# The last layer norm of a two-block transformer kernel: an extra bank, the root on other engines, smaller stores

## The chip, the core and the metric

One NeuronCore of a Trainium2 chip runs the whole program. The metric is the time of one execution on the device in microseconds (us). The engines are TensorE (PE, its weight loads PEld), VectorE (DVE), ScalarE (ACT), GpSimd (POOL) and SyncE (SP), which here only issues DMAs.

## The reference

A first transformer block and then two layers of a second one, on 256 tokens of width 1024, in float32. The second block's layers end with a gated feed-forward part and a layer norm; the change concerns only the last of these norms, the one whose result is the output.

```python
def layer_norm(x, g, b):
    mu = jnp.mean(x, axis=-1, keepdims=True)
    var = jnp.mean(jnp.square(x - mu), axis=-1, keepdims=True)
    return (x - mu) * lax.rsqrt(var + LN_EPS) * g + b

for l in range(2):
    ...
    x = layer_norm(ALPHA * x + 0.5 * swiglu(x, ffn2_w_in[l], ffn2_w_out[l]), ln_g[l, 2], ln_b[l, 2])
return x
```

## The kernel before

The 256 tokens are two tiles t=0 and t=1 of 128, tokens on the partitions. `xres` holds the residual, 128 x 2 x 1024. Every product of float32 matrices is made of three matmuls, high part by high part, high by low and low by high (`tile_mm`, L1555 to L1563), so `whi`/`wlo` are the parts of a weight block and `ht_hi`/`ht_lo` those of the hidden values. PSUM is one tensor `ps` of eight banks of 128 x 512; banks 4 to 7 gather the feed-forward output: bank 4+2t+h is tile t, columns half h. Banks 2, 3, 0 and 1 take the up projections (`up_unit`).

The program is written engine by engine, each with its own instruction stream; the order is by hand and semaphores join them. At the end of a feed-forward part `ffn_pe` finishes tile 0, then tile 1; of each it first adds the last but one unit of weights to both halves, then the last unit to half 0 and half 1. After each finished bank it raises `y_done`, after the very last one `used`. Where another norm follows, a function `late` puts transposes in front of the last product; for the last norm it is None.

`norm_dve` (L1291) is VectorE's part. For a tile, `add` (L1302) adds a bank of PSUM onto `xres` and writes the row sums to `sums`; an instruction with such a sum shows as two, the second being DVE_READ_ACCUMULATOR. `mean` (L1307) makes the negative mean `nmean` and raises `mean_ready`; `centre` (L1312) makes `cent` = (x - mean) g; `scale` (L1319) waits for `lrs`, multiplies and adds `ln_b`, in halves of 512 columns, and raises `xt_src` after each. The order is add, add, mean, centre, scale for tile 0 and then the same for tile 1. ScalarE (`norm_act`, L856) squares x - mean with a row sum into `mv`. GpSimd (`norm_pool`, `rsqrt`, L551 and L553) makes `lrs` from it: multiply and add, drain, power -0.5. ScalarE's last work before the norm are the two activations L900 of `ffn_act`. SP waits for `xt_src` and stores each half of a tile (L485, 256 KB), then waits for all four.

Of the kernel before, what the change touches and what calls it, by code (L numbers as in the profile page):

```python
# [8 lines left out]
P = 128  # L9
TOK = 256  # L10
TT = TOK // P
DM = 1024
KD = DM // P
# [9 lines left out]
LAYERS = 2  # L23
# [17 lines left out]
BW = 512  # L41
# [53 lines left out]
AHEAD = 6  # L95
ATT_ROPES = {0: (P_DQ, 0), 2: (P_DQ, 1), 4: (P_DK, 0), 6: (P_DK, 1)}
# [61 lines left out]
def build(nc, x, positions, ln1_g, w_in, q_norm_a, k_norm_a, q_norm_b, k_norm_b, sinks, w_branch_a,  # L158
# [19 lines left out]
    with ctx:  # L178
# [88 lines left out]
        nmean = little("nmean", [P, TT])  # L267
        mv = little("mv", [P, TT, 2])
# [91 lines left out]
        stored = sem("stored")  # L360
        up_tile = sem("up_tile")
# [78 lines left out]
        def _(sp):  # L440
# [40 lines left out]
            for t in range(TT):  # L481
                for h in range(2):
                    cols = slice(h * BW, (h + 1) * BW)
                    sp.wait_ge(xt_src, 4 * (XT1 + 4 * LAYERS) + 2 * t + h + 1)
                    sp.dma_start(out_r[:, t, cols], xres[:, t, cols]).then_inc(stored, 16)  # L485
            sp.wait_ge(stored, 32 * TT)
# [79 lines left out]
        def _(pool):  # L566
# [4 lines left out]
            pool.memset(half[:, :], -0.5)  # L571
            pool.memset(one_lam[:, :, :], 1.0)
# [35 lines left out]
            for l in range(LAYERS):  # L608
# [7 lines left out]
                norm_pool(pool, q + 2)  # L616
# [241 lines left out]

        def hidden_act(act, g, u, ffn):
# [43 lines left out]
        def _(act):  # L903
# [83 lines left out]
            for l in range(LAYERS):  # L987
# [49 lines left out]
                ffn_act(act, u + L_FFN2, g + FFN_S, 2 * l + 1, () if last else (u + L_UNITS, u + L_UNITS + 1))  # L1037
                for t in range(TT):
                    norm_act(act, 3 * l + 2, t)
                    if not last:  # L1040
                        xt_act(act, n + 4, toks=(t,))
# [249 lines left out]
        def norm_dve(dve, q, n, y, u, ffn, last=False):  # L1291
# [39 lines left out]
            if not last:  # L1331
                xt_dve(dve, n, toks=(0,), banks=banks, halves=(0,))
            centre(1)
            if not last:
                xt_dve(dve, n, toks=(0,), banks=banks, halves=(1,))
            scale(1)
            if not last:
                xt_dve(dve, n, toks=(1,), banks=banks)
# [48 lines left out]
        def _(dve):  # L1387
# [118 lines left out]
            for l in range(LAYERS):  # L1506
# [46 lines left out]
                norm_dve(dve, q + 2, n + 4, y + 5, u + L_UNITS - 1, True, last)  # L1553
# [407 lines left out]

        def ffn_pe(pe, u, g, f, n, late=None, banks=XT_BANKS):
# [11 lines left out]
            for t in range(TT):  # L1974
# [8 lines left out]
                for h in range(2):  # L1983
                    for k in range(2):
                        if t == h == k == 1 and late is not None:
                            late()
                        m = down_tile(pe, end, k, h, t, False, k == 1, k, par)
# [173 lines left out]
```

## Time and profile before

| | |
|---|---|
| median of 3 runs | 1321.42 us (1321.1 to 1323.9) |
| span of the profiled execution | 1321.2 us |
| PE busy | 99% of the span |
| DVE, ACT, POOL busy | 70%, 49%, 5% |
| DMA | 238.11 MB, mean 180 GB/s |
| granted clock of PE | 0.997 of full speed |

The span runs from the first to the last instruction of the profiled execution, so it is compared with the runs directly. Matmuls are pipelined: the difference of two starts is what one costs, and its own time is longer. The rows on which the prediction rests stand in a section further down.

### The profile page before, as it was taken

The numbers are of one execution on the slowest core, as the hardware profiler recorded it, in microseconds if no ns is written. First come the engines' busy times: TensorE is split into PE (matmuls) and PEld (weight loads), VectorE is DVE, ScalarE is ACT, GpSimd is POOL, SyncE is SP. The second block draws the span as 40 slices with busy tenths as digits, with TensorE's granted clock in tenths as the row PEclk, the third lists the DMA queues.
The fourth block names the chain that finished last, engine by engine and source line by source line (L and its number), as shares of the span: only waits on it lengthen the run. The fifth ranks groups of instructions, "written<-read, shape, count | busy, mean of one in ns | idle before, by whom it ended". The sixth has DMA issues, their size and how long they took to land.

```text
span 1321.2 us, 17217 instructions
## 1 busy us (share of the span) xinstructions
PE 1306.3 (99%) x6973; PEld 1102.8 (83%) x6973; DVE 925.2 (70%) x1188; ACT 640.9 (49%) x839; POOL 70.0 (5%) x145
## 2 busy tenths in 40 slices
PE   8999999999999999999999999999999999999997
PEld 7887788888888888887888888888888877888886
DVE  6698777766656666788876666776666888676665
ACT  6777635443335444457554444444443566544441
POOL 4121000000000000000300000000000003000000
PEclk9999999999999999999999999999999999999999
DMA  8543565555555555653565555465555444655550
GB/s 303 192 159 87 138 238 166 190 193 190 194 208 199 191 191 191 191 145 100 171 223 191 192 191 190 154 236 193 187 193 186 160 128 127 231 190 192 188 188 33
DMA packets 155167, 238.11 MB, mean 180 GB/s; under 512 B 4248, under 2 KB 110768, under 8 KB 155088
## 3 DMA queue, kind: packets, MB, share of 16 engines
q1 hardware_dynamic: 154704, 236.47, 54.7%
q8 instruction: 55, 0.90, 0.3%
q0 software_dynamic: 384, 0.54, 0.2%
q14 instruction: 24, 0.20, 0.0%
HBM read 235.95 MB, written 1.05 MB: 179 GB/s over the span
## 4 chain that ended last, share of the span: by engine, by line
issue 86%; PE 10%; POOL 2%; POOLq 1%; ACT 1%; DMA 0%; DVE 0%; SPq 0%; DVEq 0%; ACTq 0%
PE ps L1561 2%; PE ps L1563 2%; PE ps L1562 2%; POOLq L552 1%; POOL drs L553 1%; PE ps L1705 1%; PE ps L1628 1%; POOL lrs L553 1%; PE ps L1714 0%; DMA raw<-in_w_in_dram 0%; PE ps L1729 0%; ACT ebuf L734 0%; PE ps L1683 0%; PE ps L1603 0%; PE ps L1604 0%
## 5 line engine op out<-in xcount | busy, mean ns | idle before, releaser
L527 DVE TENSOR_TENSOR wlo<-raw,whi 128x2048 fp32r<-128x2048 f32 x172 | 391.8, 2287 | 129.2 <-ACT whi L519 129.2
L519 ACT ACTIVATE whi<-raw 128x2048 fp32r<-128x2048 f32 x197 | 369.8, 1905 | 22.3 <-DMA raw<-in_w_up_dram 11.1
L1924 PE MATMUL ps<-xt_both,whi 128*128 128x512 f32 x1504 | 358.7, 390 | 0.0
L1924 PEld LDWEIGHTS ps<-xt_both,whi 128*128 128x128 f32 x1504 | 279.1, 188 | 55.9
L1929 PEld LDWEIGHTS ps<-xt_both,wlo 128*128 128x128 f32 x1504 | 193.4, 191 | 7.6
L1241 DVE TENSOR_REDUCE hid_a<-ps 128x512 f32<-128x1024 f32 (+1 forms) x98 | 115.3, 1177 | 119.5 <-PE ps L1929 119.3
L1929 PE MATMUL ps<-xt_both,wlo 128*128 128x256 f32 x1504 | 195.7, 283 | 0.0
L1561 PE MATMUL ps<-whi,ht_hi 128*128 128x512 f32 x480 | 187.7, 391 | 0.0
L1562 PE MATMUL ps<-wlo,ht_hi 128*128 128x512 f32 x480 | 187.3, 390 | 0.0
L1563 PE MATMUL ps<-whi,ht_lo 128*128 128x512 f32 x480 | 186.8, 389 | 0.0
L877 ACT ACTIVATE hid_b<-hid_a 128x512 f32<-128x512 f32 x40 | 25.2, 631 | 236.5 <-DVE hid_a L1241 236.5
L1561 PE MATMUL ps<-whi,xt_both 128*128 128x512 f32 (+1 forms) x288 | 112.8, 392 | 0.0
L1562 PE MATMUL ps<-wlo,xt_both 128*128 128x512 f32 (+1 forms) x288 | 109.0, 378 | 0.0
L1563 PE MATMUL ps<-whi,xt_both 128*128 128x512 f32 (+1 forms) x288 | 109.0, 378 | 0.0
L1563 PEld LDWEIGHTS ps<-whi,ht_lo 128*128 128x128 f32 x480 | 90.1, 188 | 19.1
L1561 PEld LDWEIGHTS ps<-whi,ht_hi 128*128 128x128 f32 x480 | 90.3, 188 | 17.4
L1562 PEld LDWEIGHTS ps<-wlo,ht_hi 128*128 128x128 f32 x480 | 90.3, 188 | 16.8
L892 ACT ACTIVATE ht_hi<-hid_b 128x512 fp32r<-128x512 f32 x36 | 22.8, 633 | 94.1 <-DVE hid_b L1264 94.1
L500 DVE SCALAR_TENSOR_TENSOR wlo<-raw,g_cols,whi 128x512 fp32r<-128x512 f32 x80 | 56.1, 767 | 13.9 <-ACT whi L493 13.9
L1561 PEld LDWEIGHTS ps<-whi,xt_both 128*128 128x128 f32 x288 | 54.2, 188 | 12.0 <-issue 2.7
L1563 PEld LDWEIGHTS ps<-whi,xt_both 128*128 128x128 f32 x288 | 54.2, 188 | 10.4
L1562 PEld LDWEIGHTS ps<-wlo,xt_both 128*128 128x128 f32 x288 | 54.3, 189 | 8.6
(233 smaller groups left out, 1340.6 us busy)
## 6 DMA issues: line engine op xcount, KB each, us to landing
raw<-in_ffn_w_in_dram SPq DMA_DIRECT2D x80, 1024.0 KB
raw<-in_ffn_w_out_dram SPq DMA_DIRECT2D x44, 1024.0 KB
raw<-in_w_in_dram SPq DMA_DIRECT2D x36, 1024.0 KB
raw<-in_w_up_dram SPq DMA_DIRECT2D x16, 1024.0 KB
raw<-in_w_down_dram SPq DMA_DIRECT2D x16, 1024.0 KB
raw<-in_w_out_dram SPq DMA_DIRECT2D x8, 1024.0 KB
raw<-in_ffn_w_in_dram SPq DMA_DIRECT2D x16, 512.0 KB
raw<-in_w_out_dram SPq DMA_DIRECT2D x8, 512.0 KB
```

The costliest lines, as they stand in the source:

```text
L500: m = dve.scalar_tensor_tensor(wlo[j][:, cols], raw[j][:, cols], g_cols[:, k:k + 1], whi[j][:, cols].bitcast(F32), ALU.mult, ALU.subtract)
L519: act.activation(whi[j][:, :], raw[j][:, :], ACT.Copy).then_inc(hi_done, 1)
L527: dve.tensor_tensor(wlo[j][:, :], raw[j][:, :], whi[j][:, :].bitcast(F32), ALU.subtract).then_inc(lo_done, 1)
L553: pool.tensor_tensor(dst, dst, half[:, 0:dst.shape[-1]], ALU.pow).then_inc(done, 1)
L877: act.activation(hid_b[:, 0, :], hid_a[:, 0, :], ACT.Silu).then_inc(hid_act, 2)
L892: act.activation(ht_hi[s % 2][:, 0:2, :], hidden2, ACT.Copy).then_inc(ht_hi_done, 2)
L1241: return dve.tensor_reduce(hid_a[:, j, k * TOK:(k + n) * TOK].rearrange("p (k n) -> p k n", k=n), ps[:, b:b + n, :].rearrange("p k (j n) - ...
L1561: pe.matmul(o, hi[:, k, tok], block_of(whi, u, b, width), start=start, stop=False)
L1562: pe.matmul(o, hi[:, k, tok], block_of(wlo, u, b, width), start=False, stop=False)
L1563: return pe.matmul(o, lo[:, k, tok], block_of(whi, u, b, width), start=False, stop=stop)
L1924: pe.matmul(o(k).rearrange("p (j n) -> p j n", j=2), whi[w][:, block(b, k)], xt_both[:, :, b, :], start=b == 0, stop=False)
L1929: m = pe.matmul(o(k)[:, 0:TOK], wlo[w][:, block(b, k)], xt_hi[:, b, :], start=False, stop=b == KD - 1)
```

## The change

Only the last norm (layer 1, second feed-forward part) changes.

- TensorE: the last product (tile 1, half 1, last unit of weights) is done in two quarters of 256 columns. The first goes on in bank 7 and raises `y_done`, the second starts anew in bank 0 and raises `used`; it is the only one for its columns in that bank, so bank 7 holds what came before it.
- VectorE has a function of its own. Of tile 1 it adds 512 columns, 256 and 256 from bank 6 and 7, sums two quarters' totals, and adds the 256 columns from bank 0 last, whose total replaces that of the third add. A mean divided by 32 as well goes to ScalarE; a second instruction makes the mean proper. `factor` waits for `var_ready` and takes a reciprocal in place of the wait for GpSimd.
- ScalarE squares with scale 1/32, so that the sum is the variance, drains, and takes the root with `eps2` as bias. A small Sqrt stands ahead of both tiles.
- GpSimd sets the constant `eps2` and leaves out its last `norm_pool`.
- Stores: five pieces, two of tile 0 (512 columns each), three of tile 1 (512, 256 and 256 columns), each waiting for `rows_out`.

```diff
+LAST_PIECES = ((0, slice(0, BW)), (0, slice(BW, DM)), (1, slice(0, BW)), (1, slice(BW, DM - BW // 2)),
+               (1, slice(DM - BW // 2, DM)))
...
-            for t in range(TT):
-                for h in range(2):
-                    cols = slice(h * BW, (h + 1) * BW)
-                    sp.wait_ge(xt_src, 4 * (XT1 + 4 * LAYERS) + 2 * t + h + 1)
-                    sp.dma_start(out_r[:, t, cols], xres[:, t, cols]).then_inc(stored, 16)
-            sp.wait_ge(stored, 32 * TT)
+            for i, (t, cols) in enumerate(LAST_PIECES):
+                sp.wait_ge(rows_out, i + 1)
+                sp.dma_start(out_r[:, t, cols], xres[:, t, cols]).then_inc(stored, 16)
+            sp.wait_ge(stored, 16 * len(LAST_PIECES))
...
+            pool.memset(eps2[:, :], EPS2 / ALPHA ** 2)
...
-                norm_pool(pool, q + 2)
+                if l < LAYERS - 1:
+                    norm_pool(pool, q + 2)
...
+        def last_norm_act(act, q, t):
+
+            act.wait_ge(mean_ready, 2 * q + t + 1)
+            act.activation(squares[:, t, :], xres[:, t, :], ACT.Square, bias=nmean_root[:, t:t + 1], scale=1.0 / ROOT_DM,
+                           accum_out=mv[:, t, 1:2])
+            act.drain()
+            act.activation(lrs[:, t:t + 1], mv[:, t, 1:2], ACT.Sqrt, bias=eps2[:, 0:1]).then_inc(var_ready, 1)
...
+                if last:
+                    act.activation(scratch[:, :], ident[:, 0:1], ACT.Sqrt)
                 for t in range(TT):
-                    norm_act(act, 3 * l + 2, t)
-                    if not last:
+                    if last:
+                        last_norm_act(act, 3 * l + 2, t)
+                    else:
+                        norm_act(act, 3 * l + 2, t)
                         xt_act(act, n + 4, toks=(t,))
...
+        def last_norm_dve(dve, q, y, u):
+
+
+            def add(t, a, z, src, total, *ready):
+                xs = xres[:, t, a:z]
+                dve.wait_ge(*ready)
+                dve.scalar_tensor_tensor(xs, src, 0.5 / ALPHA, xs, ALU.mult, ALU.add, accum_out=total)
+
+            def mean(t, first, second):
+                dve.drain()
+                dve.tensor_scalar(nmean_root[:, t:t + 1], first, second, -1.0 / (DM * ROOT_DM),
+                                  ALU.add, ALU.mult).then_inc(mean_ready, 1)
+                dve.tensor_scalar(nmean[:, t:t + 1], first, second, -1.0 / DM, ALU.add, ALU.mult)
+                dve.drain()
...
+            def factor(t):
+                dve.wait_ge(var_ready, 2 * q + t + 1)
+                m = dve.reciprocal(lrs[:, t:t + 1], lrs[:, t:t + 1])
+                dve.drain()
+                return m
+
+            def scale(t, cols):
+                dve.scalar_tensor_tensor(xres[:, t, cols], cent[:, t, cols], lrs[:, t:t + 1], ln_b[:, cols],
+                                         ALU.mult, ALU.add).then_inc(rows_out, 1)
...
+            centre(0)
+            factor(0)
+            for t, cols in LAST_PIECES[:2]:
+                scale(t, cols)
+            add(1, 0, BW, ps[:, 6, :], quarter[:, 0:1], y_done, y + 3)
+            add(1, BW, DM - BW // 2, ps[:, 7, 0:BW // 2], quarter[:, 1:2], y_done, y + 4)
+            add(1, DM - BW // 2, DM, ps[:, 7, BW // 2:BW], quarter[:, 3:4], y_done, y + 4)
+            dve.drain()
+            dve.tensor_tensor(quarter[:, 2:3], quarter[:, 0:1], quarter[:, 1:2], ALU.add)
+            add(1, DM - BW // 2, DM, ps[:, 0, 0:BW // 2], quarter[:, 3:4], used, u + 1)
+            mean(1, quarter[:, 2:3], quarter[:, 3:4])
+            centre(1)
+            dve.drain()
+            factor(1)
+            for i, (t, cols) in enumerate(LAST_PIECES[2:]):
+                scale(t, cols)
...
+        def last_columns(pe, u, par):
+
+            tok = slice(P, TOK)
+            for q, o in enumerate((ps[:, 7, 0:BW // 2], ps[:, 0, 0:BW // 2])):
+                for k in range(2):
+                    a = (2 * k + 1) * BW + q * BW // 2
+                    hi, lo = (w[SLOT_OF[u]][:, a:a + BW // 2] for w in (whi, wlo))
+                    pe.matmul(o, ht_hi[par][:, k, tok], hi, start=q == 1 and k == 0, stop=False)
+                    pe.matmul(o, ht_hi[par][:, k, tok], lo, start=False, stop=False)
+                    m = pe.matmul(o, ht_lo[par][:, k, tok], hi, start=False, stop=k == 1)
+                m.then_inc(y_done if q == 0 else used, 1)
...
+                    if t == h == 1 and late is None:
+                        last_columns(pe, end, par)
+                        break
```

## Rows read from the trace of the kernel before

**Rows 1.** The page, part 1: busy time, share and instructions of each engine.

```profile
PE 1306.3 (99%) x6973; PEld 1102.8 (83%) x6973; DVE 925.2 (70%) x1188; ACT 640.9 (49%) x839; POOL 70.0 (5%) x145
```

**Rows 2.** Busy time by stretch, for PE, PEld, DVE, ACT, POOL; then clock, DMA share, GB/s.

```profile
1314.00:1317.30 3.30, 0.00 (x1) 0.00 (x0) 2.31 (x6) 1.24 (x2) 0.69 (x2) 0.87 0.37 138
1317.30:1321.20 3.90, 0.00 (x0) 0.00 (x0) 1.41 (x2) 0.00 (x0) 0.05 (x1) 0.50 0.37 137
```

**Rows 3.** The chain of work that ended last: start, us, what.

```profile
1316.78 0.58 POOLq L178
...
1317.38 0.75 DVE xres L1319
```

**Rows 4.** The timeline of PE: start, us, engine, line, operation; the last six matmuls.

```profile
1312.48 0.39 PE L1561 MATMUL ps<-whi,ht_hi 128*128 128x512 f32 x1
...
1313.61 0.39 PE L1563 MATMUL ps<-whi,ht_lo 128*128 128x512 f32 x1
```

**Rows 5.** The timeline of DVE, with idle time before in brackets.

```profile
1312.17 1.41 DVE L1319 SCALAR_TENSOR_TENSOR xres<-cent,lrs,ln_b 128x512 f32<-128x512 f32 x2 [1.20 <-POOL lrs L553]
1313.51 0.68 DVE L1302 SCALAR_TENSOR_TENSOR xres<-ps,xres 128x512 f32<-128x512 f32 x1
...
1314.12 0.68 DVE L1302 SCALAR_TENSOR_TENSOR xres<-ps,xres 128x512 f32<-128x512 f32 x1
1314.73 0.08 DVE L1302 DVE_READ_ACCUMULATOR xres<-ps,xres 128x1 f32 x1
1314.89 0.21 DVE L1307 TENSOR_SCALAR nmean<-sums 128x1 f32<-128x1 f32 x1
```

**Rows 6.** The timeline of ACT.

```profile
1304.38 0.42 ACT L900 ACTIVATE ht_hi<-hid_b 128x256 fp32r<-128x256 f32 x1 [2.39 <-DVE hid_b L1286]
1309.63 1.15 ACT L856 ACTIVATE squares<-xres,nmean 128x1024 f32<-128x1024 f32 x1 [4.83 <-DVE nmean L1307]
1310.68 0.19 ACT L856 ACTIVATION_READ_ACCUMULATOR squares<-xres,nmean 128x1 f32 x1
...
1316.19 0.19 ACT L856 ACTIVATION_READ_ACCUMULATOR squares<-xres,nmean 128x1 f32 x1
```

**Rows 7.** Small instructions: ns min/median/max of one line, and DVE's timeline.

```profile
L739 ACT ACTIVATE esink<-sink,ntop x16: 279/286/292, 127.6 to 149.1; 128x1 f32<-128x1 f32 x16
...
97.72 0.15 DVE L1065 TENSOR_SCALAR ntop<-top 128x1 f32<-128x1 f32 x1
97.79 0.15 DVE L1080 RECIPROCAL rden<-den 128x1 f32<-128x1 f32 x1
98.02 0.42 DVE L1082 TENSOR_SCALAR ebuf<-ebuf,rden 128x384 f32<-128x384 f32 x1
```

**Rows 8.** Timelines of DVE and PE where instructions have 256 columns.

```profile
1044.33 0.43 DVE L1115 TENSOR_TENSOR proj<-rope 128x256 f32<-128x256 f32 x1
1044.67 0.42 DVE L1116 TENSOR_TENSOR proj<-rope 128x256 f32<-128x256 f32 x1
...
1299.19 1.12 PE L1929 MATMUL ps<-xt_both,wlo 128*128 128x256 f32 x8
1300.14 0.40 PE L1924 MATMUL ps<-xt_both,whi 128*128 128x512 f32 x1
```

**Rows 9.** The last store: issue, time to landing; stretches with DMA share, GB/s last.

```profile
1318.82 0.33 SPq L485 DMA_DIRECT2D out_dram<-xres  x1
...
DMA to landing us min/median/max: 2.0/2.0/2.0
...
1318.90:1319.20 0.30, 0.00 (x0) 0.00 (x0) 0.00 (x0) 0.00 (x0) 0.00 (x0) 0.50 0.67 253
...
1320.00:1320.30 0.30, 0.00 (x0) 0.00 (x0) 0.00 (x0) 0.00 (x0) 0.00 (x0) 0.50 1.03 396
```

**Rows 10.** Table loads and the squares of the norms, over the span.

```profile
L882 ACT ACT_TABLE_LOAD  x3: 1283/1283/1283, 383.5 to 1141.2; - x3
...
L856 ACT ACTIVATE squares<-xres,nmean 128x1024 f32<-128x1024 f32 x12 | 13.8, 1153 | 29.8 <-DVE nmean L1307 29.8
```

## What the change is forecast to do

> **What bounds the kernel now.** I read the page's busy shares first [rows 1]: TensorE has 99% of the span, so over most of it nothing but TensorE's work counts, and this change leaves all of that work alone up to its last block. What it touches lies at the very end, so the next view is the busy time by stretch [rows 2]. Between 1314.0 and 1317.3 us the matmul count is down to its last one, and VectorE, ScalarE and GpSimd take turns; what comes after 1317.3 is 1.41 us of VectorE and then only the store. The chain of work [rows 3] gives the order in that tail: GpSimd's step for the root ends just ahead of 1317.38, and VectorE's last multiply starts at that moment. So the end is a serial path of small instructions, some 7 us long, behind the last matmul. Only steps on it are worth anything.
>
> The path in detail, for the second token tile (t=1): the last matmul starts at 1313.61 and lasts 0.39, so TensorE ends at 1314.00 [rows 4]. VectorE could have begun its adds before, but is busy with the scaling of tile 0 until 1313.51, which it began only when GpSimd delivered at 1312.17; its two adds of 512 columns start at 1313.51 and 1314.12, the sum is read at 1314.73, and the mean M starts at 1314.89 [rows 5]. ScalarE squares after that and has its sum read out at 1316.19+0.19 = 1316.38, M+1.49 [rows 6]. Then GpSimd, and the scaling, which I call S, at 1317.38 = M+2.49 [rows 3]. Two halves of the tile are scaled and stored; the last store is issued at 1318.82, has landed 2.0 us later (1320.82), and the span ends at 1321.2, about 0.4 behind [rows 9].
>
> The changed part is thus a few tenths of a us in 1321.2. Comparisons of this kernel tell about 0.2% (2.6 us) from no change, and nothing on this path adds up to that unless a step of over 2 us goes or comes.
>
> **Root by ScalarE, inverse by VectorE.** Removed: from 1316.38 to 1317.38, 1.00 us (two instructions of GpSimd and the handings over) [rows 3, 6]. Added: a drain of ScalarE, Sqrt on 128x1, a handing over, a reciprocal on 128x1, a drain. No row shows a Sqrt; the nearest is an activation on 128x1 with a pointer operand, 0.286 us [rows 7]. The drain I take at 0.08, the gap that VectorE shows between the end of a sum's readout (1314.73+0.08) and the mean that needs it (1314.89) [rows 5]; the handing over at 0.03. Reciprocal to dependent instruction, drain included: 97.79 to 98.02, 0.23 [rows 7]. Sum 0.08+0.29+0.03+0.23 = 0.63, so S comes at M+1.49+0.63 = M+2.12 instead of M+2.49: 0.37 gained. Bounds: with no gap at the ScalarE drain 0.45, with a gap of 0.4 there a gain of 0.05. VectorE's `nmean` is now written by a second instruction behind the one that releases ScalarE. That moves centring (1.28 us) from M+0.31 to about M+0.4; it ends near M+1.7, before the Sqrt does at M+1.86, so it is covered and costs nothing. Were the cover gone it would cost 0.1.
>
> The same edit for tile 0: its sum is read out by 1310.68+0.19 = 1310.87 [rows 6], so scaling starts at 1311.50 where it started at 1312.17, 0.67 earlier. That is not on the end by itself; what it gives is that VectorE gets sooner to the adds of tile 1. Two scalings take 1.34 (1312.17 to 1313.51), so VectorE is free at 1312.84. Bank 6 is complete by then: the block before the last one has its last matmul 0.23 ahead of 1312.48, and 0.39 later it is 1312.64 [rows 4].
>
> **A bank of its own for the last 256 columns.** Without this edit the early start would be worth little: add 1 at 1312.84, but add 2 must wait for TensorE at 1314.00+0.04, its sum is read from 1314.65 on, M = 1314.81, a gain of 0.08. The edit lets VectorE take 768 of the 1024 columns while TensorE works on the last 256. On TensorE six matmuls of 512 columns become twelve of 256. A matmul of 256 columns in this trace follows its neighbour after 0.12: eight of them from 1299.19 to 1300.14 [rows 8]. They write another tile and load other weights, but have the same sizes. Twelve take 1.42 instead of 1.36, with the last one starting at 1312.48+11x0.12 = 1313.80 and lasting about 0.28: TensorE ends at 1314.08, 0.08 later. The first six are complete at about 1313.36.
>
> VectorE: add 1 (512 columns) 1312.84 to 1313.45; add 2 (256 columns) may start then, since its bank is ready at 1313.40. A pair of 256-column instructions is 0.34 apart, where a pair of 512 columns is 0.61 apart [rows 5, 8], so halving the columns doesn't halve the time. Add 3 starts at 1313.79, its sum is read from 1314.13 to 1314.21, the drain puts the little sum of two quarters at 1314.29, and add 4 follows 0.07 later (the spacing of 97.72 and 97.79 [rows 7]) at 1314.36, with TensorE long done. Readout to 1314.78, drain, M = 1314.86. That is 0.03 before the 1314.89 of now and 0.05 after the 1314.81 that the faster root would give alone. VectorE, not TensorE, is the late one: this edit buys nothing. Bounds for M against now: 0.1 earlier, 0.15 later if each 256-column add with its readout takes 0.4 instead of 0.34.
>
> The Trainium skill has a rule against it. VectorE: DVE Perf Modes, section "The TRN2 errata — SBUF-src ops pay a fixed extra latency per instruction", says that the fixed cost sits between instructions and that tiles should have 512 elements or more. The rows agree in kind, 0.34 against half of 0.61; by them the fixed part of an instruction is 0.07.
>
> **Stores in smaller pieces.** S is now M+2.12 = 1316.98, 0.40 earlier. Tile 1 was two pieces of 256 KB, issued at S+0.78 and S+1.44; it becomes 256, 128 and 128 KB. VectorE: the second scaling starts at S+0.67, the third 0.40 later (256 columns fewer than 0.67, at the 0.27 by which 0.61 and 0.34 differ), and ends near S+1.55; last issue S+1.58, 0.14 later than now. SP takes 0.33 per issue [rows 9], less than the 0.40 between pieces, so it doesn't queue. What the last piece gains depends on the DMA engines. Their share is 0.67 in the first 0.3 us from 1318.9 and 1.03 up to 1320.3 [rows 9]; over the 3.9 us from 1317.3 it is 0.37, which is 1.44 us of full engines [rows 2]. From 1318.93 (S+1.55) that reaches to about 1320.4 (S+3.0), so there is no gap between the two pieces. If the bytes decide, cutting them does nothing, the first piece's issue at S+0.78 is what counts, and the landing stays at S+3.44; packets of half the size may cost 0.05 to 0.1. If the time from issue to landing decides, the last 128 KB lack half of some 0.7 of transfer: 2.0-0.35 = 1.65, landing at S+1.58+1.65 = S+3.23, 0.21 better. I take the first, since the rows show the engines full, with 0.07 for the smaller packets.
>
> **Off the path.** A preload of the Sqrt table goes behind ScalarE's last activation before the norm, which ends at 1304.80; ScalarE then waits 4.83 us for the mean [rows 6]. A table load takes 1.28 and a little activation 0.2 to 0.3 [rows 7, 10]: hidden, and without that cover it would cost 1.6. The constant `eps2` costs one small instruction of GpSimd at the start, which then waits for work of other engines. The stores of tile 0 land more than 4 us before the end; SP waits for them before those of tile 1, as now, and nothing else is queued on SP. GpSimd has no more work and no one waits for it.
>
> **Sum.** M 0.03, root 0.37, pieces -0.07: 0.33 off the span of 1321.2, which lies 0.2 under the median of the runs, 1321.42. I forecast 1321.42-0.33 = 1321.1.
>
> **Rivals.**
> - The landing decides, not the bytes: 0.07 more is not lost and 0.21 gained, together 0.6 off, 1320.8. For it: 2.0 us from issue to landing with 0.7 of transfer in it. Against: full DMA engines.
> - No net gain: the drain of ScalarE takes 0.4 and the 256-column adds 0.4 each, M 0.15 later and root 0.05: 1321.5. For it: neither pairing has a row of its own.
> - Slower, by table loads. If the table that holds Sqrt doesn't hold Square, a load stands between each Square and its Sqrt. One mechanism, at one place: 1.28 on tile 0 delays the scaling, the adds and M by the same, and 1.28 more comes before S. 2.56 on top of 1321.1 is 1323.7; if the load before each Square is exposed too, twice that, 1326.2. It decides as soon as one load lies after 1309.6. Against it: twelve Squares on this line have run behind Silu or Exp with no load on the line [rows 10], so Square comes with the other tables. The Trainium skill, ScalarE: Activation LUTs, section "What ACT_TABLE_LOAD costs", puts a switch with its drain at about 2.66 us, by which this case would be 1326.4; the load's own 1.283 is what this trace shows.
> - The bank doesn't do what it says (argued above): included in the forecast, as M hardly moves. If it does, because the small sums overlap the readout, M is 0.1 earlier: 1321.0.
>
> **How the numbers follow.** The forecast with its bounds 0.62, landing rival 0.16, no net gain 0.12, table loads 0.05, and 0.05 for something neither view shows. The cases but the table loads lie between 1320.4 and 1321.6. The three runs of now spread from 1321.1 to 1323.9, and a median of few runs can fall high in that; the range therefore is 1320.4 to 1322.9, leaving out the table loads and the highest of such medians. Faster by over 0.2% (below 1318.8) 0.02, needs a gain of four times the largest bound. Slower by over 0.2% (above 1324.1) 0.04: the exposed table loads and half of the unknown. Within it 0.94.
>
> **What would show it.** Right: Sqrt 0.08 behind the readout and about 0.29 long; reciprocal to scaling 0.23; S-M = 2.1; M at 1314.9 with VectorE busy without a gap from 1311.5 on; TensorE ending at 1314.1; DMA share near 1 for 1.4 us without a gap, and the last landing about 3.5 behind S. Wrong: a table load after 1309.6, a wait of VectorE for TensorE in front of the last add, a DMA share that drops between the pieces, or a last store that lands in 1.7 us.

## The result, and the profile after

The changed kernel takes 1323.86 us (median of 21 runs, 1322.97 to 1326.3); beside it the kernel before took 1321.8 (21 runs, 1321.1 to 1324.22). The ratio is 1.0016, 95% interval 1.001 to 1.0023: slower, by less than the 0.2% that the prediction called a difference, but by 2.1 us where 0.33 us less was forecast, and above the top of the range, 1322.9. The profiled execution has a span of 1323.4 where it was 1321.2.

**The end, where the change lies.** VectorE's timeline from the first add of the last norm on (columns as in [rows 5]), first one row of before as the common mark, then the kernel after:

```profile
1307.24 0.69 DVE L1302 SCALAR_TENSOR_TENSOR xres<-ps,xres 128x512 f32<-128x512 f32 x1 [1.99 <-PE ps L1563]
```

```profile
1309.33 0.69 DVE L1365 SCALAR_TENSOR_TENSOR xres<-ps,xres 128x512 f32<-128x512 f32 x1 [1.99 <-PE ps L1634]
...
1313.64 0.16 DVE L1379 RECIPROCAL lrs<-lrs 128x1 f32<-128x1 f32 x1 [0.46 <-ACT lrs L875]
1313.88 1.42 DVE L1384 SCALAR_TENSOR_TENSOR xres<-cent,lrs,ln_b 128x512 f32<-128x512 f32 x2
1315.21 0.68 DVE L1365 SCALAR_TENSOR_TENSOR xres<-ps,xres 128x512 f32<-128x512 f32 x1
...
1316.75 0.42 DVE L1365 SCALAR_TENSOR_TENSOR xres<-ps,xres 128x256 f32<-128x256 f32 x1
...
1317.25 0.21 DVE L1369 TENSOR_SCALAR nmean_root<-quarter 128x1 f32<-128x1 f32 x1
...
1319.14 0.16 DVE L1379 RECIPROCAL lrs<-lrs 128x1 f32<-128x1 f32 x1 [0.18 <-ACT lrs L875]
1319.39 1.54 DVE L1384 SCALAR_TENSOR_TENSOR xres<-cent,lrs,ln_b 128x512 f32<-128x512 f32 x3
```

The first add waits in both kernels for the same matmul, and it already comes 2.09 us late (1309.33 against 1307.24). From there to the end of the span it is 1323.4 - 1309.33 = 14.1 us, where it was 1321.2 - 1307.24 = 14.0. So the part of the program that the change rewrites is 0.1 slower, and the 2 us are lost before it, in work that the change doesn't touch. ScalarE's rows of the same stretch:

```profile
1306.90 1.28 ACT L1057 ACT_TABLE_LOAD   x1
1308.20 0.20 ACT L1057 ACTIVATE scratch<-ident 128x1 f32<-128x1 f32 x1
1311.72 1.15 ACT L872 ACTIVATE squares<-xres,nmean_root 128x1024 f32<-128x1024 f32 x1 [3.32 <-DVE nmean_root L1369]
1312.78 0.18 ACT L872 ACTIVATION_READ_ACCUMULATOR squares<-xres,nmean_root 128x1 f32 x1
1313.31 0.29 ACT L875 ACTIVATE lrs<-mv,eps 128x1 f32<-128x1 f32 x1 [0.35 <-issue]
...
1318.55 0.19 ACT L872 ACTIVATION_READ_ACCUMULATOR squares<-xres,nmean_root 128x1 f32 x1
1318.81 0.30 ACT L875 ACTIVATE lrs<-mv,eps 128x1 f32<-128x1 f32 x1
```

The table load is hidden: behind it ScalarE still waits 3.32 us for the mean, and no other load follows. The first Sqrt stands 0.35 behind the readout (1312.78+0.18 = 1312.96) with nothing to wait for ("issue"), the second only 0.07 behind it. TensorE, timeline, first and last of the twelve matmuls of 256 columns:

```profile
1314.57 0.28 PE L2040 MATMUL ps<-whi,ht_hi 128*128 128x256 f32 x1
...
1315.89 0.28 PE L2042 MATMUL ps<-whi,ht_lo 128*128 128x256 f32 x1
```

**The start, where the time went.** Matched matmul by matmul, the two traces are 2 us apart from the 40th microsecond on and stay so. Waits for each engine from 15 to 45 us (us in total, times, longest), first before, then after:

```profile
POOL lrs L551 <- issue: 1.0, 1, 1.0
ACT proj L653 <- POOL lrs L553: 0.3, 1, 0.3
```

```profile
POOL lrs L559 <- issue: 5.1, 1, 5.1
ACT proj L663 <- POOL lrs L561: 4.5, 1, 4.5
DVE pos_f L1412 <- DMA dlam<-in_diff_lambda_dram: 2.6, 1, 2.6
...
PE ps L1632 <- ACT proj L663: 2.1, 1, 2.1
```

GpSimd's first root of the program (that of another, earlier norm) comes late, ScalarE waits for it, and TensorE, which waited for nobody in this stretch before, waits 2.1 us for ScalarE. GpSimd's timeline, the first root, before and after:

```profile
23.31 0.77 POOL L551 TENSOR_SCALAR lrs<-mv 128x1 f32<-128x1 f32 x1 [1.05 <-issue]
```

```profile
26.70 0.18 POOL L559 TENSOR_SCALAR lrs<-mv 128x1 f32<-128x1 f32 x1 [5.10 <-issue]
```

What had changed by then are DMAs. GpSimd's queue loads ten small constants at the start, broadcast to the 128 partitions. The DMA issues up to 45 us (what, queue, count, KB, us from issue to landing), before and after:

```profile
dlam<-in_diff_lambda_dram POOLq DMA_DIRECT2D x1, 256.0 KB, 3.9
...
sink<-in_swa_sink_dram POOLq DMA_DIRECT2D x1, 8.0 KB, 4.0
```

```profile
dlam<-in_diff_lambda_dram POOLq DMA_DIRECT2D x1, 256.0 KB, 8.0
...
sink<-in_swa_sink_dram POOLq DMA_DIRECT2D x1, 8.0 KB, 6.4
```

The same bytes, from the same queue, take up to twice as long. The slow ones are those of the second block: `dlam`, the sub-norm's gain (6.8 us for 3.9) and the second block's sinks; the first block's four gains stay at 4.3 to 5.2 us. In all 17 traces of this study in which GpSimd's queue carried such loads, slow or not, its first root started 0.50 to 0.87 us behind the last landing of that queue. Between the issues and the root the program has 42 small instructions, which run at once (18.68 to 21.60 in after), and then a `drain` of GpSimd. So the wait lies at or behind this `drain`; that it is the `drain` which waits for the landings is likely, but no run takes it out or moves it. Stretches of the span (busy time of PE, PEld, DVE, ACT, POOL, then clock, DMA share, GB/s), before and then after:

```profile
8.00:12.00 4.00, 3.00 (x7) 2.18 (x8) 3.02 (x5) 4.00 (x8) 0.00 (x0) 0.64 1.05 411
...
20.00:24.00 4.00, 4.00 (x18) 3.00 (x17) 4.00 (x7) 4.00 (x8) 2.95 (x26) 1.00 0.67 159
```

```profile
20.00:24.00 4.00, 4.00 (x18) 3.08 (x17) 3.58 (x6) 4.00 (x8) 1.60 (x5) 1.00 0.76 80
...
32.00:36.00 4.00, 1.93 (x7) 1.50 (x7) 4.00 (x6) 4.00 (x8) 2.92 (x5) 0.90 0.77 260
36.00:40.00 4.00, 4.00 (x13) 3.13 (x12) 3.63 (x7) 3.98 (x7) 0.00 (x0) 0.67 0.15 59
```

From 20 to 24 us the DMA engines are busy to 0.76 and move 80 GB/s; before they were busy to 0.67 and moved 159. From 15 to 30 us GpSimd's queue has the same 384 packets and 0.54 MB in before and in p3 (a run below, before with an unused Sqrt), but they occupy the engines for 16.8% of that time in before and 28.3% in p3: these packets themselves take longer.

Behind TensorE's wait its granted clock falls to the lower level (1.2 GHz) for 3.4 us, with 13 matmuls in 36 to 40 us where 19 is usual. Before has such a stretch too, but at 9.1 to 12.5 us, behind a wait of TensorE for its first weights that is longer than in a trace with neither loss (s1, below). TensorE's timeline at this place, before and then s1:

```profile
8.99 3.73 PE L1628 MATMUL ps<-whi,xt_both 128*128 128x512 f32 x8 [1.98 <-ACT whi L493]
```

```profile
8.01 1.20 PE L1630 MATMUL ps<-whi,xt_both 128*128 128x512 f32 x4 [1.09 <-ACT whi L493]
```

This early loss comes and goes in traces of both kinds: those of x1 and p2 lose 1.3 us at this wait with no stretch of lower clock, x2 and x3 (x3 with Sqrt) 2.9 with one. The later stretch, near 36 us, stands only in traces with a late root, and there behind waits of 2.1 to 2.5 us (after, s2, x4); f1 and g1 have waits of 2.2 and 3.0 and no such stretch. So it may be a further cost of the change in some executions. Matmul number 500 (counted from 0) starts at 107.87 in s1, at 109.69 in before and at 111.84 in after. Before has lost 1.8 against s1, 1.0 of it at the wait for its first weights and 0.8 by the lower clock; after has lost 4.0, of which 2.2 are the wait for the root and 1.7 the lower clock.

### The profile page after: what moved, and what is told of

Its sections match the earlier page's. It is cut to its first block, busy times and chain, and to the rows that moved or that the text cites. A ratio compares the mean times of both kernels' runs of the same rounds, so it can differ in the third digit from the quotient of the medians.

```text
span 1323.4 us, 17243 instructions
## 1 busy us (share of the span) xinstructions
PE 1306.4 (99%) x6979; PEld 1102.8 (83%) x6979; DVE 926.7 (70%) x1198; ACT 642.9 (49%) x843; POOL 67.5 (5%) x142
## 4 chain that ended last, share of the span: by engine, by line
issue 71%; PE 23%; POOL 2%; ACT 1%; POOLq 1%; DMA 1%; DVE 1%; SPq 0%; DVEq 0%; ACTq 0%
PE ps L1995 6%; PE ps L1632 4%; PE ps L1634 4%; PE ps L1633 4%; PE ps L2000 3%; POOLq L560 1%; POOL drs L561 1%; PE ps L1776 1%; DMA raw<-in_w_in_dram 1%; POOL lrs L561 0%; PE ps L1785 0%; PE ps L1800 0%; ACT ebuf L744 0%; ACT whi L501 0%; PE ps L1754 0%
```

## The experiments

Ratios are to the kernel before, run beside each group; "lowest span" is the shortest span of the runs of a kernel (8 to 11 of a variant, 21 of after, 25 to 31 of before, which favours before a little). It is the least touched by the losses at the start that come and go. For before it was 1319.0 to 1319.3 each time, for after 1320.8.

**First, what of the change is enough: addresses, one more instruction, or neither.** The change allocates three small tensors, and everything behind them moves by 96 bytes; and GpSimd gets a memset ahead of the start's work. x1 is before with the three tensors, unused:

```diff
+        nmean_root = little("nmean_root", [P, TT])
+        quarter = little("quarter", [P, 4])
+        eps2 = little("eps2", [P, 1])
```

x2 is before with the memset and its tensor:

```diff
+        eps2 = little("eps2", [P, 1])
...
+            pool.memset(eps2[:, :], EPS2 / ALPHA ** 2)
```

x3 is the change with the three tensors of x1 allocated behind all others, x4 the change with the memset moved behind the start's other work on GpSimd.

> The kernel before with the three small tensors of the change allocated at their place in SBUF and never used, so that everything allocated after them, the constants that GpSimd loads among it, lies 96 bytes further on. No instruction is added. Theory placement (the broadcast constants land at addresses that are no longer multiples of 64 bytes, their packets take longer, GpSimd's first root waits for them): some 2 us slower, about 1323.8, the last GpSimd packet landing near 25.7 us and TensorE's clock at half for one stretch near 36. Theory extra instruction (the added constant moves GpSimd's instruction stream) and theory tail: no change, about 1321.5.

> The kernel before with the constant eps2 set by GpSimd at the start, its tensor allocated behind all others so that nothing moves. Theory extra instruction: some 2 us slower, GpSimd idle about 5 us before its first root. Theory placement: no change, 1321.5, GpSimd idle about 1 us there.

> The changed kernel with its three small tensors allocated behind all others. Theory placement: the start is that of the kernel before, the tail gains what its own trace shows, so 1321.0 to 1321.6. Theory extra instruction: still 1323.8.

> The changed kernel with eps2 set by GpSimd behind its first roots in place of the very start; the small tensors stay where the change puts them. Theory placement: still 1323.8. Theory extra instruction: 1321.3.

Measured: x1 1322.45 us, ratio 1.0001 (0.9992 to 1.0011); x2 1323.2, 1.0005 (0.9996 to 1.0014); x3 1324.12, 1.0012 (1.0002 to 1.0021); x4 1324.34, 1.0016 (1.0007 to 1.0025); before beside them 1322.39. The landing of `dlam` took 3.9, 4.0, 5.7 and 8.6 us. Both theories fell: neither the addresses nor the memset make before slow, and taking either out of the change doesn't mend it (lowest spans 1319.5 and 1319.3 for x1 and x2, 1321.2 and 1321.3 for x3 and x4). x3's trace has a root at 25.42, 2 us later than before's, and yet no wait of TensorE for it: TensorE had already lost 2.9 us against s1 by matmul 45, more than the root was late, so in this trace the late root cost it nothing.

**Second, the three parts of the change.** p3 is before with nothing but an unused Sqrt ahead of the last norm:

```diff
+                if last:
+                    act.activation(scratch[:, :], ident[:, 0:1], ACT.Sqrt)
```

p1 has the root alone: it is the change with four stores and tile 1 added in two halves, banks 6 and 7 as before:

```diff
-            add(1, 0, BW, ps[:, 6, :], quarter[:, 0:1], y_done, y + 3)
...
-            add(1, DM - BW // 2, DM, ps[:, 0, 0:BW // 2], quarter[:, 3:4], used, u + 1)
+            add(1, 0, BW, ps[:, 6, :], sums[:, 1, 0:1], y_done, y + 3)
+            add(1, BW, DM, ps[:, 7, :], sums[:, 1, 1:2], used, u + 1)
```

p2 has bank and pieces, with GpSimd's root kept:

```diff
-                if l < LAYERS - 1:
-                    norm_pool(pool, q + 2)
+                norm_pool(pool, q + 2)
...
-                dve.wait_ge(var_ready, 2 * q + t + 1)
-                m = dve.reciprocal(lrs[:, t:t + 1], lrs[:, t:t + 1])
...
+                dve.wait_ge(lrs_ready, 2 * q + t + 1)
```

p4 has the pieces alone, that is before with the loops over `LAST_PIECES` in VectorE's scaling and in SP's stores.

> The kernel before with one thing added: the small Sqrt activation in ScalarE's idle time ahead of the last norm. Nothing reads its result. It brings one table load of 1.28 us, hidden under a wait of 4.8 us, and makes Sqrt's table one more that the program needs. Theory table set (a program with one more table starts later or slower, whatever uses the table): 1.5 to 2.5 us slower, the time outside the span 0.3 to 0.4 longer, GpSimd's constants landing 2 us or more later. Theory tail, and theory of code layout at the end: no change, time outside the span 1.8.

> The changed kernel with the root given back to GpSimd: the extra bank, the split adds and the smaller stores stay, no Sqrt is anywhere. Theory table set: start and time outside the span as in the kernel before, so 1321.5 to 1323, no slower than 0.3 beyond it. Theory code layout (any added instructions on TensorE, VectorE and SP shift it): still some 2 us slower.

> The changed kernel with the bank and the smaller stores undone: root by ScalarE and inverse by VectorE alone. Theory table set: 1.5 to 2 us slower than before, with a tail behind the last unit of weights that is 0.3 to 0.5 shorter than that of the kernel before. Theory code layout: about as before, or 0.4 faster.

> Only the smaller stores of the last tile, root and bank undone. If the bytes decide, as predicted: the tail 0.05 to 0.1 longer. If the time from issue to landing decides: 0.2 shorter. Start as in the kernel before under both theories of the start.

Measured: p3 1324.05 us, ratio 1.0009 (0.9999 to 1.0018), lowest span 1320.8; p2 1323.11, 1.0005 (0.9996 to 1.0015), 1319.9; p1 1323.59, 1.0013 (1.0004 to 1.0022), 1320.9; p4 1322.82, 1.0 (0.9991 to 1.001), 1319.5; before 1321.92, 1319.0. The two with Sqrt have the late start, the two without it don't: the landing of `dlam` was 7.4 and 8.0 us against 3.9 and 3.9, the first root at 25.69 and 26.34 against 23.55 and 23.35. p3's interval alone doesn't part it from no change; its lowest span (1.8 above before's) and its trace do. One activation, hidden 1300 us further on, costs the start some 2 us.

The tails of these traces part the three terms of my sum. VectorE's timeline of p1:

```profile
1307.36 0.69 DVE L1364 SCALAR_TENSOR_TENSOR xres<-ps,xres 128x512 f32<-128x512 f32 x1 [1.99 <-PE ps L1629]
...
1314.16 0.69 DVE L1364 SCALAR_TENSOR_TENSOR xres<-ps,xres 128x512 f32<-128x512 f32 x1 [0.21 <-PE ps L1629]
...
1314.94 0.21 DVE L1368 TENSOR_SCALAR nmean_root<-sums 128x1 f32<-128x1 f32 x1
...
1317.07 1.41 DVE L1383 SCALAR_TENSOR_TENSOR xres<-cent,lrs,ln_b 128x512 f32<-128x512 f32 x2
```

And of p2, bank and pieces with the old root:

```profile
1306.75 0.69 DVE L1359 SCALAR_TENSOR_TENSOR xres<-ps,xres 128x512 f32<-128x512 f32 x1 [1.99 <-PE ps L1624]
...
1313.00 0.68 DVE L1359 SCALAR_TENSOR_TENSOR xres<-ps,xres 128x512 f32<-128x512 f32 x1
...
1315.04 0.21 DVE L1363 TENSOR_SCALAR nmean<-quarter 128x1 f32<-128x1 f32 x1
...
1317.53 1.54 DVE L1374 SCALAR_TENSOR_TENSOR xres<-cent,lrs,ln_b 128x512 f32<-128x512 f32 x3 [0.89 <-POOL lrs L561]
```

Each counted from its own first add F, with the mean's start M, the last scaling's start S and the end of the span E as differences of rows:

| kernel | M-F | S-M | E-S | E-F |
|---|---|---|---|---|
| before (F 1307.24, [rows 3, 5]) | 7.65 | 2.49 | 3.8 | 14.0 |
| p1, root | 7.58 | 2.13 | 3.8 | 13.5 |
| p4, pieces | 7.64 | 2.49 | 4.0 | 14.2 |
| p2, bank and pieces | 8.29 | 2.49 | 4.1 | 14.9 |
| after | 7.92 | 2.14 | 4.0 | 14.1 |

(p4's rows are 1307.44, 1315.08, 1317.57 and a span of 1321.6; spans are printed to 0.1.) The root gains 0.07+0.36 = 0.43 (p1's M-F of 7.58 is the 7.57 that the prediction gave to the root alone). The pieces lose 0.2. The bank loses 0.64 by itself and 0.34 on top of the root.

**Third, which activations do it.** p3 again with another function: in s1 Exp, whose table the program loads anyway, in s2 Gelu, which needs another, as Sqrt does.

```diff
-                    act.activation(scratch[:, :], ident[:, 0:1], ACT.Sqrt)
+                    act.activation(scratch[:, :], ident[:, 0:1], ACT.Gelu)
```

> The kernel before with a small Exp activation, whose result nothing reads, in ScalarE's idle time ahead of the last norm, where the Sqrt stood in the run with Sqrt alone. It brings the same 1.28 us table load at the end, but of a table that the program uses anyway. Theory new table (what counts is a table that the program didn't have): as before, 1321.9, slowest GpSimd packet about 1 us, last one by 23 us. Theory one more load (any load at the end of one execution disturbs the start of the next): some 1.6 us slower, packets up to 1.4 to 2.5 us.

> The same with a small Gelu, which no other place of the program uses. Theory new table: some 1.6 us slower, like Sqrt alone, slowest GpSimd packet 1.4 us or more, last one landing at 24.5 us or later. Theory Sqrt (something of that function alone): as before, 1321.9.

Measured: s1 1321.55 us, ratio 0.9999 (0.9989 to 1.0008), lowest span 1319.1, as before's; s2 1324.04, 1.0014 (1.0005 to 1.0024), 1321.3. GpSimd's first root, s1 and then s2:

```profile
22.75 0.19 POOL L551 TENSOR_SCALAR lrs<-mv 128x1 f32<-128x1 f32 x1 [1.29 <-issue]
```

```profile
27.11 0.18 POOL L551 TENSOR_SCALAR lrs<-mv 128x1 f32<-128x1 f32 x1 [5.61 <-issue]
```

s1 has a table load at this place too, as ScalarE's timeline shows:

```profile
1303.02 1.28 ACT L1039 ACT_TABLE_LOAD   x1
1304.32 0.20 ACT L1039 ACTIVATE scratch<-ident 128x1 f32<-128x1 f32 x1
```

So it is neither the added activation nor the added load of a table, but one more table set in the program.

**Fourth, does it help to take the loads off GpSimd's queue?** If the slowness were that queue's, SP should load them at the usual speed. In f1 (p1 with it) and f2 (before with it) SP loads `dlam` and `subg` between its strips of weights; in g1, g2 and g3 (p1, before and the whole change) SP loads all ten there. Of f1's edit, the lines for `dlam`; the loads of the weight units 4 and 5 stood in a loop and are written out, in the same order:

```diff
+            load(sp, 4, rows_of(4), w_in_r[:, 0:4, 2 * BW:3 * BW])
...
+            sp.dma_start(dlam[:, :, :, :], diff_lambda_2.partition_broadcast(P)).then_inc(sp_loaded, 16)
+            load(sp, 5, rows_of(5), w_in_r[:, 4:8, 2 * BW:3 * BW])
...
-            pool.dma_start(dlam[:, :, :, :], diff_lambda_2.partition_broadcast(P)).then_inc(const_loaded, 16)
```

> Root by ScalarE and inverse by VectorE alone, and the two large broadcast constants (lambda vectors and the sub-norm's gain, 384 KB) loaded from SP behind the fifth unit of weights in place of from GpSimd at 17.6 us. Theory slow GpSimd packets (the start is long since GpSimd's first root waits for its own constants): the first root comes at 22.5 to 23.5 us, TensorE has no wait in front of the third strip, spans some 1.6 us below those of the root-only kernel; with a tail 0.4 shorter it is 0.3 to 1 us faster than the kernel before, about 1321.3. Theory that the first root's delay hides nothing else (TensorE's loss comes from the weights): no change against the root-only kernel, 1323.6.

> The kernel before with the same two loads moved to SP. Theory slow GpSimd packets: its first root already waits only about 1 us, and moves by that at most; 0 to 0.7 us faster, with fewer runs in the upper group (spans above 1321). Otherwise no change, 1321.9.

> Root by ScalarE and inverse by VectorE alone, and all ten constants of the start loaded by SP behind the fifth unit of weights, so that GpSimd issues no DMA at all. Theory A (a program with one table more has slow packets in GpSimd's queue, and these are the whole way by which the start gets longer): GpSimd's first root 1 us behind the square that it needs, near 23, no wait of TensorE in front of the third strip, median span 2 us under the root-only kernel's 1321.8; with a tail 0.42 shorter than now 1320.5 to 1321.5, faster than the kernel before. Theory B (the packets are slow in whatever queue they are, what is slow being small packets or their source): constants landing at 24 us or later, 1323.6 as with the root alone.

> The kernel before with all ten constants loaded by SP. Theory A: GpSimd's first root about where it is, as it is bound by the square by then; 0 to 0.5 us faster than before, and 0.4 us slower than the same with the root by ScalarE. Theory B: the same or slower, since SP issues ten more DMAs.

> The whole change with all ten constants loaded by SP. Theory A: the start of the kernel before with the change's tail, which is 0.1 longer than now: 0.5 slower than the root-only kernel with the same loads, so 1321.2 to 1322.2. Theory B: 1323.9 as the change itself.

Measured: f1 1324.15 us, ratio 1.001 (1.0001 to 1.002), and f2 1322.88, 1.0 (0.9991 to 1.001); g1 1324.16, 1.0017 (1.0008 to 1.0026); g2 1321.95, 0.9999 (0.999 to 1.0008); g3 1325.9, 1.0029 (1.0019 to 1.0039). What I expected of f1 was missed: `dlam` landed only 14.9 us after its issue, the second block's sinks, still in GpSimd's queue, 9.2 us, and the first root came at 27.48. In f2 `dlam` took 10.6 too, with no Sqrt, so a landing in SP's queue behind these strips is no clean measure. (f2's sinks, in GpSimd's queue, took 4.9.) g3 came out 2 us above the higher of its two expectations; its trace loses 1.3 us at the first weights and 2.0 at TensorE's later wait, and 0.7 of its excess over before lies outside the span (below). g1 and g2 decide. Landings in SP's queue, g2 (no Sqrt) and then g1 (Sqrt):

```profile
dlam<-in_diff_lambda_dram SPq DMA_DIRECT2D x1, 256.0 KB, 5.4
```

```profile
dlam<-in_diff_lambda_dram SPq DMA_DIRECT2D x1, 256.0 KB, 9.1
```

In g1 GpSimd's two first roots are on time (15.21 and 21.51), and TensorE waits all the same, for weights that stand behind the slow loads. The waits of g1 from 15 to 45 us:

```profile
ACT whi L512 <- DMA raw<-in_w_in_dram: 3.3, 1, 3.3
PE ps L1630 <- DVE wlo L519: 3.0, 1, 3.0
```

In g2 ScalarE waits 0.7 for these weights and TensorE for nobody. The slowness isn't the queue's. It goes with the loads.

**Fifth, the loads' source, or how many there are?** h1 is p1 with one edit: the second block's sinks, sub-norm gain and lambda vectors are read from slices of the layer norm's bias input, in the same sizes, at the same places of the program and of GpSimd's queue. (These constants then have other values, so h1 doesn't compute the reference; the work is the same.) h2 and h3 (p1 and before) have SP load `dlam` and `subg` behind the fourth strip of weights, and what reads them comes three strips later. Of h1's edit, the line for `dlam`:

```diff
-            pool.dma_start(dlam[:, :, :, :], diff_lambda_2.partition_broadcast(P)).then_inc(const_loaded, 16)
+            pool.dma_start(dlam[:, :, :, :].rearrange("p l j n -> p (l j n)"), ln_b_2[0, 0, 0:512].partition_broadcast(P)).then_inc(const_loaded, 16)
```

> The root-only kernel with three of GpSimd's ten constants (second block's sinks, sub-norm gain, lambda vectors) read from slices of the layer norm bias in place of their own inputs, with the same sizes and places in SBUF; the second block's attention is computed from those wrong constants, all other work is as before. Theory source (the packets that read these small inputs are slow where the program has one table more, because of where the inputs then lie): packets of at most 1.1 us, lambda vectors landing 4 us after their issue, GpSimd's first root near 23, about 1321.3. Theory time (any broadcast read in that stretch is slow then): packets of 1.4 to 2.5 us, landing 7 to 8 us, first root at 25 or later, 1323.6.

> The root-only kernel with the two large constants loaded by SP behind the fourth strip of weights, and what reads them moved three strips later on VectorE and ScalarE. Theory A (the start is long only because small constants and the first weights queue behind these slow packets): first root near 23, no wait of TensorE in front of the third strip, tail 0.42 shorter: 1320.8 to 1321.6, faster than the kernel before by 0.2 to 1 us. Theory C (the slow packets hit whatever is loaded at the time): the third or a later strip waits instead, 1322.5 to 1324.

> The same deferral in the kernel before, as a control: 0 to 0.5 us faster, 1321.5; 0.4 slower than with the root by ScalarE if theory A holds.

Measured: h1 1321.1 us, ratio 0.9997 (0.9988 to 1.0006), median span 1319.3 and lowest 1318.8, where before had 1319.6 and 1319.1. The same load in h1, and the first root:

```profile
dlam<-in_ln_b_dram POOLq DMA_DIRECT2D x1, 256.0 KB, 4.8
```

```profile
23.75 0.21 POOL L558 TENSOR_SCALAR lrs<-mv 128x1 f32<-128x1 f32 x1 [1.91 <-issue]
```

With Sqrt in the program, and only the source of three loads changed, the start is as before. h1 differs from p1 in one thing more, which no run parts from this: the three small inputs are no longer read at all. Its spans are 0.3 under before's, as the root's 0.43 at the end would have it, though the ratio can't part that from no change. h2 took 1324.34, 1.0015 (1.0006 to 1.0024), h3 1323.54, 1.0013 (1.0004 to 1.0021). h2's expectation was missed by its median. Its trace is as hoped, with the root at 23.49, no wait of TensorE in the stretch and a `dlam` landing of 5.8 us; but its spans lie in two heaps, five at 1319.4 to 1320.2 and six at 1322.1 to 1322.6, and the trace is of the lower one. That h3, without Sqrt, loses as much by its median shows that the move has a price of its own. A part of it has a place, which both traces show: TensorE waits 0.47 us for VectorE at 96.20 (h3) and 95.38 (h2), in front of a product of the attention, where s1 has no wait. It is about what h3's lowest span has over before's (1319.5 against 1319.1). The rest stays open. No version that does the whole reference beat the kernel before.

## Why the prediction was wrong

**The step that failed** is the paragraph "Off the path". It priced the Sqrt ahead of the norm as a table load and a small activation, hidden in a wait of 4.83 us, that is at nothing. That stands for the place where the instruction runs: load 1.28, activation 0.20, 3.32 us of wait left. What I didn't ask is what a further table set changes for the program as a whole, and I looked at no row of the start. There it costs about 2 us: p3 against before in lowest span 1.8, p3 and s2 by median 2.1 and 2.3 (against 1321.92 and 1321.74), s1 nothing. Shown are these links: a further set, Sqrt's or Gelu's, in the program (p3, s2; not s1); slow broadcast reads of those small inputs, in either queue (g1, g2) and gone when another input is read (h1); GpSimd's first root 2 to 5 us late (or, in SP's queue, the weights); TensorE idle for 1.2 to 2.5 us (p3 1.2, p1 1.8, after 2.1, s2 2.3, x4 2.5), except in x3, where it was late already, and in h2.

What is only argued is why these inputs become slow; that the runtime places inputs in device memory in another way when a program brings more tables would fit, but no run reads addresses there. Nor was a cheap cure tried: taking out or moving the `drain` in front of GpSimd's first root, so that the root needn't stand behind the loads. The Trainium skill, ScalarE: Activation LUTs, section "What ACT_TABLE_LOAD costs", says that all sets of a program are brought by DMA to the engine's backing slots when the model starts; the runs here show only that a further set changes the start, not how. And the Trainium skill, DMA: Bandwidth & Descriptors, section "Latency and other measured facts", has copies between large arrays run at half the rate by nothing but their row pitch, the mechanism being an inference there too. No run here has such copies; h1's 4.8 against p1's 8.0 us may be another case of a rate that hangs on where the source lies.

My rival "slower, by table loads" gave 1323.7 and the time is 1323.86, but that is chance: no load stands between Square and Sqrt.

**The rest of the 2.1 us.** By median, after's spans are 1321.7 and its runs 2.16 longer than their spans; for before it is 1.8. So 0.35 of the loss lies outside the first and last instruction. A further table set alone doesn't bring it: p1, p3 and s2 have 1.8, though 0.3 to 0.4 more had been expected of p3. But it comes together with one in most cases: after has 2.16 and p2, the same without Sqrt, 1.81; f1 2.23 and f2 1.81; h2 2.25 and h3 1.80; g1 2.15 and g2, without Sqrt, 2.02; x3 and x4 have 2.16, g3 2.51. So in these pairs nearly all of it comes where Sqrt's set and some further edit stand together; what in the edit does it stays open.

**Root: right.** S-M was forecast at 2.12 and is 2.14 (p1 2.13); the second drain is 0.07 for my 0.08, Sqrt 0.30 for 0.29, reciprocal to scaling 0.25 for 0.23. Sum 0.37 forecast, 0.35 measured.

**Bank: right in kind, mis-sized by 0.3.** TensorE's twelve matmuls follow at 0.12 as forecast (1314.57 to 1315.89). VectorE's four adds run without a wait, and from the first of tile 1 to M they take 2.04 (1315.21 to 1317.25) for the 2.02 of the sum. But that first add was forecast at 1312.84, F+5.60, and comes at F+5.88 (1315.21-1309.33). The missing 0.28 are one row: the first Sqrt's 0.35 of "issue", for which I had put 0.08. The second Sqrt has 0.07, so the gap belongs to the first time, not to the drain; p1 shows it too (0.36). I had given the drain of ScalarE a bound of 0.4, but used it for S alone and not for tile 0, where the gap really is. In p1 it is covered, since VectorE waits 0.21 for TensorE in front of the second add in any case. With the split there is no such wait: VectorE, busy throughout, carries every delay to M. Thus the bank, forecast 0.05 worse than the root alone, was 0.34 worse. (That the gap comes with the first time is read from the rows; what the engine does in it no view shows.) And where the root is GpSimd's, add 1 starts when VectorE is free and the split costs its full price, 0.64 (p2).

**Pieces: right in kind, mis-sized by 0.1.** The forecast was that the bytes decide and that smaller packets cost 0.07, a figure that no row stood behind. p4 and after show 0.2. The DMA engines of after, in stretches of 0.3 us with share and GB/s last:

```profile
1321.20:1321.50 0.30, 0.00 (x0) 0.00 (x0) 0.00 (x0) 0.00 (x0) 0.00 (x0) 0.50 1.00 369
...
1322.10:1322.40 0.30, 0.00 (x0) 0.00 (x0) 0.00 (x0) 0.00 (x0) 0.00 (x0) 0.50 1.00 335
```

There is no gap between the pieces, and at a full share the engines move 335 to 369 GB/s, where with halves alone they moved 375 to 396 (at 1319.2 to 1320.3 in before, the last of it in [rows 9]). A last piece of 128 KB lands 2.1 us after its issue, a half of 256 KB took 2.0 [rows 9], so the rival "the landing decides" fell.

**The sum of the end**: M 0.27 later, root 0.35 earlier, E-S 0.2 later, 0.1 worse; forecast 0.33 better. **The range** failed by what it covered: every bound was one of the end's own steps, and 0.05 for "something neither view shows" was too little for a kernel whose TensorE is busy at 99%, where a wait of TensorE early on goes whole into the time. The spread that I had read as chance in three runs (1321.1 to 1323.9) is of the size of the early loss, the wait for the first weights and the lower clock behind it, which traces show as 0 to 2.9 us.

## What to carry to other kernels

Before an activation of a new table set is added for some tenths of a microsecond, compare the start of the program too: run the kernel with the bare activation and look at when the first loads land and when each engine's first real work begins. Measure a change of a few tenths by rows counted from a mark that both kernels share, since the whole may move for a reason that lies 1300 us away. And a cost that is covered in one version of a path (the cold Sqrt behind TensorE's last block) comes out when another edit takes the cover away: bound it at each place where it occurs, not only at the last.

## What the runs showed of the hardware

- With a further table set in the program, in p3 and s2 that of one unused activation, a 256 KB broadcast load issued near 18 us took 7.4 to 8.6 us in place of 3.9 to 4.2 (p3, p1, s2, x4 and after, against before, x1, x2, p2, p4 and s1; x3 5.7). In after the engines' share was 0.76 at 80 GB/s, in before 0.67 at 159.
- The first instruction of GpSimd behind a `drain` started 0.50 to 0.87 us behind the last landing of its own queue's loads, in 17 traces, while 42 instructions ahead of the `drain` ran at once: in after the root came at 26.70 with 5.10 us of "issue", 0.60 behind that landing; in g1, where SP had the loads, at 15.21 with 0.19 of "issue".
- The first Sqrt on the variance stood 0.34 to 0.36 us idle with nothing to wait for, in nine traces, the second about 0.07, although a Sqrt into `scratch` had gone before.
- The table load took 1.28 us with no gap of note on either side: the activation before it ended at 1306.89, the load ran from 1306.90, the next activation began at 1308.20. The Trainium skill (ScalarE: Activation LUTs, "What ACT_TABLE_LOAD costs") adds a drain of 1.38 to a switch; here the measurement decides, and no such time is seen.
